# Softmax passes of an attention pipeline stand one unit later in ScalarE's and VectorE's order, between two copies of turned probabilities

## The chip, the cores and the metric

One core of a Trainium2 chip. TensorE (PE in the profile), VectorE (DVE), ScalarE (ACT), GpSimd (POOL) and SyncE (SP) each work through an instruction stream of their own, in the order in which the kernel wrote it, and wait for each other with semaphores. The metric is the device time of one execution in microseconds.

## The reference, cut to what matters

One encoder block on 1024 tokens of 1024 channels, float32. A first part mixes tokens in two attention branches with 8 heads each, a second part is a mixture of 32 experts. The attention is what the change touches:

```python
# branch B ("fox"): causal, each head has keys and values of its own
logit = jnp.einsum('bqhd,bshd->bhqs', q_blk, kb) * ATTN_SCALE
logit = logit + cq_blk - cum_t            # bias, then the causal mask
p = jax.nn.softmax(logit, axis=-1)
ob = jnp.einsum('bhqs,bshd->bqhd', p, vb)
# branch A ("dsa"): one key head and one value head for all, 256 selected keys per query
logit = jnp.where(valid, logit, NEG_INF)
p = jax.nn.softmax(logit, axis=-1)
oa = jnp.einsum('bqhk,bqkd->bqhd', p, v_sel)
```

## The kernel before

All work orders are written out by hand. The time from about 218 to 714 us is a pipeline over 64 **units**. A unit is one pair of heads (p, 0 to 3) and one block b of 128 queries, which looks at b+1 tiles of 128 keys. Units 0 to 31 are branch B, and in each pair b runs 7, 6, 5, ..., 0. Units 32 to 63 are branch A, and in each pair b runs 7, 0, 6, 1, 5, 2, 4, 3. "Block 7" below is a unit with b = 7: its rows are 1024 wide, those of block 4 are 640 wide, those of block 0 are 128 wide.

The stages of one unit are these, each for the two heads z = 0 and 1:

- scores: PE multiplies queries by keys into PSUM (L1120).
- `largest`: DVE adds bias or mask, writes the logits to SBUF and takes the row extremum (L1600, semaphore `lg_done`).
- `exps`: ACT takes the exponential in place and sums the row (L810, `p_done`).
- `inverse`: DVE takes the reciprocal of the two sums (L1607, `r_ok`).
- `scaled`: each row is multiplied by it (`n_done`), on ACT in branch B (L816), on DVE in branch A (L1614).
- turning: PE transposes the probabilities into one of two PSUM banks, in groups of two key tiles times two heads, so of up to four 128x128 tiles (L1131). Block 7 and block 6 have 4 groups, blocks 5 and 4 have 3, 3 and 2 have 2, 1 and 0 have 1.
- `turned`: ACT copies each group to SBUF (L823, `pt_copied`).
- values: PE multiplies the values by each copied group (L1145, `pv_done`).
- The output is copied from PSUM by ACT in branch B (L855) and by DVE in branch A (`out_a`, L1619, `o_done`). The first values product of the next unit waits for that.

Each engine has a loop over n from -3 to 63 (LEAD is 3), and one pass handles several units. In pass n PE issues the scores of unit n+3, then the turning of unit n, where the values of a group follow the turning of the group after it:

```python
for f in range(groups):
    turn_p(n, f)
    if f >= 1:
        values(n, f - 1)
```

Between them and the last values product PE has other work in some passes: projections of the next head pair (L1095, L1101) in units of branch B other than blocks 3 and 1 of the first three pairs, query projections and turns of branch A (L1159, L1167, rotated on DVE at L1648 to L1651) in units 24 to 32, and modulation rows (L1176, added on DVE at L1664) in units 44 to 51. The scores of a unit wait until `largest` of the unit before it is done.

In pass n ACT copies the groups of unit n. In branch B one of the two `scaled` of unit n+2 stands behind each of the first two copies. Behind the last copy stand the two `exps` of unit n+3. In passes 56 to 62 a rounding of 1024 columns follows (`high`, L843), whose counterpart on DVE is `low` (L1672, passes 57 to 63).

In pass n DVE does, in branch A, the output copy of unit n-1, `inverse` and `scaled` of unit n+2, `largest` of unit n+3, and then pieces of other work. In branch B it does `largest` of unit n+3, half of the pieces of a threshold search (L1535), `inverse` of unit n+3, and the other half. `choose` (L1635 to L1639) is such a piece, in passes 28 to 33.

Of the kernel before, what the change touches and what calls it, by code (L numbers as in the profile page):

```python
# [22 lines left out]
TT = S // P  # L23
# [48 lines left out]
LEAD = 3  # L72
# [50 lines left out]
def build(nc, x, c, positions, w_mod, b_mod, g_mix, w_in, b_forget, w_out_a, w_out_b, w_out, g_ffn,  # L123
# [11 lines left out]
    with ExitStack() as ctx:  # L135
# [315 lines left out]
        def logits(n):  # L451
            return (lg_b if n < N_B else lg_a)[n % 4]
# [265 lines left out]
        def _(act):  # L718
# [83 lines left out]
                    dst = vall[p % 2][:, 4 * half:4 * half + 4, :].rearrange("q a n -> q (a n)")  # L802
                act.activation(dst, ps[:, 7, :], ACT.Copy, scale=float(HD ** -0.5) if j == 1 else 1.0).then_inc(pj_out, 1)

            def exps(n):
                b = UNITS[n][2]
                for z in range(2):
                    buf, u = logits(n)[z][:, 0:WB[b]], 2 * (n % TT) + z
                    act.wait_ge(lg_done, 2 * n + z + 1)
                    act.activation(buf, buf, ACT.Exp, bias=nmax[:, u:u + 1], scale=-1.0, accum_out=rs[:, u:u + 1]).then_inc(p_done, 1)  # L810

            def scaled(n, z):
                b = UNITS[n][2]
                buf, u = logits(n)[z][:, 0:WB[b]], 2 * (n % TT) + z
                act.wait_ge(r_ok, n + 1)
                act.activation(buf, buf, ACT.Copy, scale=rinv[:, u:u + 1]).then_inc(n_done, 1)  # L816
# [34 lines left out]
            for n in range(-LEAD, N_U):  # L851
                if 1 <= n <= N_B:
                    _, p, b = UNITS[n - 1]
                    act.wait_ge(pv_done, GROUP_AT[n])
                    act.activation(oT[1][p][:, b * P:(b + 1) * P], ps[:, 6, 0:P], ACT.Copy).then_inc(o_done, 1)  # L855
                left = [0, 1] if 0 <= n + LEAD - 1 < N_B else []
                if n >= 0:
                    for f in range(len(key_groups(n))):
                        turned(n, f)
                        if left:  # L860
                            scaled(n + LEAD - 1, left.pop(0))
                for z in left:
                    scaled(n + LEAD - 1, z)
                if N_B - TT < n <= N_B:
                    qa_turned(n - (N_B - TT) - 1)
                if n + LEAD < N_U:
                    exps(n + LEAD)
                if -3 <= n < -1:
                    pj_evac(0, n + 7)
                elif 0 <= n < N_B - TT and n % TT in PJ_AT:  # L870
                    pj_evac(n // TT + 1, PJ_AT[n % TT])
                elif N_B - TT <= n < N_B:
                    qa_copy(n - (N_B - TT))
                if n >= N_U - TT and n - (N_U - TT) < KT - 1:
                    high(n - (N_U - TT))
# [491 lines left out]
        def _(dve):  # L1367
# [236 lines left out]
            def inverse(n):  # L1604
                u = 2 * (n % TT)
                dve.wait_ge(p_done, 2 * n + 2)
                dve.reciprocal(rinv[:, u:u + 2], rs[:, u:u + 2]).then_inc(r_ok, 1)  # L1607
# [77 lines left out]
            for n in range(-LEAD, N_U):  # L1685
                todo = parts.get(n, [])
                if n > N_B:
                    out_a(n - 1)
                if N_B - TT < n <= N_B:
                    rope_a(n - (N_B - TT) - 1)  # L1690
                if N_B <= n + LEAD - 1 < N_U:
                    inverse(n + LEAD - 1)
                    scaled(n + LEAD - 1)
                if n + LEAD < N_U:
                    largest(n + LEAD)
                half = len(todo) // 2 if n + LEAD < N_B else 0
                for piece in todo[:half]:
                    piece()
                if n + LEAD < N_B:
                    inverse(n + LEAD)  # L1700
                for piece in todo[half:]:
                    piece()
            out_a(N_U - 1)
# [242 lines left out]
```

## Time and profile before

| | |
|---|---|
| median of 3 runs | 1828.5 us (1826.37 to 1828.74) |
| the profiled execution | 1829.64 us, its span 1827.4 us |
| PE busy | 1676.7 us, 92% of the span |
| DVE busy | 961.7 us, 53% |
| ACT busy | 496.6 us, 27% |

The profiled execution's own time is its span and 2.2 us around it. The span holds, in this order, the projections (to 218 us), the pipeline of units (to 714 us), the output projections and gates, the routing, and the experts (from about 1300 us).

### The profile page before, as it was taken

The numbers are of one execution on the slowest core, as the hardware profiler recorded it, in microseconds if no ns is written. First come the engines' busy times: TensorE is split into PE (matmuls) and PEld (weight loads), VectorE is DVE, ScalarE is ACT, GpSimd is POOL, SyncE is SP. The second block draws the span as 40 slices with busy tenths as digits, with TensorE's granted clock in tenths as the row PEclk, the third lists the DMA queues.
The fourth block names the chain that finished last, engine by engine and source line by source line (L and its number), as shares of the span: only waits on it lengthen the run. The fifth ranks groups of instructions, "written<-read, shape, count | busy, mean of one in ns | idle before, by whom it ended". The sixth has DMA issues, their size and how long they took to land.

```text
span 1827.4 us, 22908 instructions
## 1 busy us (share of the span) xinstructions
PE 1676.7 (92%) x7928; PEld 857.0 (47%) x7929; DVE 961.7 (53%) x1913; ACT 496.6 (27%) x1020; POOL 191.1 (10%) x371
## 2 busy tenths in 40 slices
PE   5998889999998898999999999499999989999892
PEld 2563456564644555676666455233333333333330
DVE  5666697887877665556464433533333323333323
ACT  3214545454544655101110112011111111111112
POOL 0010000000000000000000000122222212222221
PEclk9999999999999999999999998699999999999996
DMA  9552201010000120112111813899999746999996
GB/s 353 184 187 67 70 19 40 24 47 1 1 1 2 58 70 1 35 34 69 34 34 70 324 58 109 328 357 398 378 327 400 283 126 233 395 401 368 397 400 246
DMA packets 102905, 316.63 MB, mean 173 GB/s; under 512 B 9920, under 2 KB 46824, under 8 KB 78256
## 3 DMA queue, kind: packets, MB, share of 16 engines
q1 hardware_dynamic: 91088, 287.88, 41.0%
q0 software_dynamic: 11744, 27.79, 6.3%
q8 instruction: 44, 0.72, 0.2%
q14 instruction: 29, 0.24, 0.0%
HBM read 289.14 MB, written 26.51 MB: 173 GB/s over the span
## 4 chain that ended last, share of the span: by engine, by line
PE 83%; DVE 5%; ACT 5%; DMA 4%; issue 2%; SPq 1%; POOLq 0%; POOL 0%; DVEq 0%; ACTq 0%
PE ps L1296 19%; PE ps L1222 10%; PE ps L1314 9%; PE ps L1211 6%; PE ps L1095 5%; PE ps L1257 5%; PE ps L1145 4%; PE ps L1120 4%; PE ps L1015 3%; PE ps L1159 3%; PE ps L1131 2%; PE ps L1101 2%; ACT arena L823 2%; PE ps L1053 2%; PE ps L1290 2%
## 5 line engine op out<-in xcount | busy, mean ns | idle before, releaser
L1296 PE MATMUL ps<-arena 128*64 128x512 f32 x1632 | 377.2, 605 | 17.0 <-issue 10.1
L1296 PEld LDWEIGHTS ps<-arena 128*64 128x64 f32 x1632 | 115.6, 139 | 231.7 <-issue 217.8
L1884 DVE COPY arena<-ps 128x256 f32<-128x256 f32 x51 | 21.6, 424 | 381.9 <-ACT arena L931 381.9
L1314 PE MATMUL ps<-arena 128*64 128x512 f32 x816 | 186.3, 598 | 0.6 <-DVE arena L1906 0.6
L1222 PE MATMUL ps<-rounded 128*128 128x512 f32 x768 | 183.3, 398 | 0.0
L1535 DVE TENSOR_SCALAR_CACHE_REDUCE arena<-arena,small 128x384 bf16<-128x384 f32 (+2 forms) x192 | 171.3, 939 | 0.0
L1222 PEld LDWEIGHTS ps<-rounded 128*128 128x128 f32 x768 | 144.2, 188 | 36.6 <-issue 7.7
L710 POOL DMA_INDIRECT sum_rows<-arena,ones x51 | 81.4, 1595 | 433.3 <-DVE arena L1906 422.3
L1145 PE MATMUL ps<-arena 128*64 128x128 f32 x1152 | 96.4, 286 | 23.4 <-ACT arena L823 22.4
L1211 PE MATMUL ps<-arena 128*128 128x512 f32 x256 | 112.5, 592 | 2.2 <-DVEq L1708 2.2
L1257 PE MATMUL ps<-arena 128*128 128x512 f32 x256 | 112.0, 595 | 1.9 <-DMA arena<-in_w_out_dram 1.9
L1600 DVE CUSTOM_DVE_ANT_0 arena<-ps,arena 128x896 f32<-128x896 f32 (+7 forms) x128 | 91.7, 753 | 39.9 <-PE ps L1120 37.5
L935 ACT ACTIVATE arena<-ps 128x256 f32<-128x256 f32 x51 | 19.5, 383 | 336.7 <-PE ps L1305 336.7
L823 ACT ACTIVATE arena<-ps 128x512 f32<-128x512 f32 (+1 forms) x160 | 85.4, 551 | 88.5 <-PE ps L1131 88.3
L1714 DVE RECIPROCAL arena<-arena 128x1024 f32<-128x1024 f32 x16 | 104.8, 6553 | 0.5
L810 ACT ACTIVATE arena<-arena,small 128x896 f32<-128x896 f32 (+7 forms) x128 | 97.8, 769 | 12.0 <-DVE small L1600 12.0
L1314 PEld LDWEIGHTS ps<-arena 128*64 128x64 f32 x816 | 54.3, 136 | 94.0 <-issue 88.0
L1145 PEld LDWEIGHTS ps<-arena 128*64 128x64 f32 x1152 | 59.7, 136 | 71.2 <-ACT arena L823 45.5
L1120 PE MATMUL ps<-arena 64*128 64x512 f32 (+3 forms) x384 | 81.2, 528 | 11.6 <-DVE small L1600 10.7
L1889 DVE RECIPROCAL arena<-arena 128x256 f32<-128x256 f32 x51 | 89.0, 1745 | 0.0
L1131 PE MATMUL ps<-ident,arena 128*128 128x128 f32 x576 | 88.7, 286 | 0.0
L890 ACT ACTIVATE arena<-ps 128x1024 f32<-128x1024 f32 x16 | 16.4, 1023 | 256.0 <-PE ps L1222 256.0
(297 smaller groups left out, 2012.7 us busy)
## 6 DMA issues: line engine op xcount, KB each, us to landing
arena<-in_w_e_gate_dram SPq DMA_DIRECT2D x64, 1024.0 KB
arena<-in_w_e_up_dram SPq DMA_DIRECT2D x64, 1024.0 KB
arena<-in_w_e_down_dram SPq DMA_DIRECT2D x32, 2048.0 KB
arena<-in_w_mod_dram SPq DMA_DIRECT2D x12, 2048.0 KB, 8.5
arena<-in_w_in_dram SPq DMA_DIRECT2D x32, 512.0 KB, 4.5
arena<-in_x_dram SPq DMA_DIRECT2D x16, 512.0 KB, 8.4
sum_rows<-arena SPq DMA_DIRECT2D x9, 512.0 KB, 2.6
arena<-cum_rows SPq DMA_DIRECT2D x8, 512.0 KB, 5.2
```

The costliest lines, as they stand in the source:

```text
L810: act.activation(buf, buf, ACT.Exp, bias=nmax[:, u:u + 1], scale=-1.0, accum_out=rs[:, u:u + 1]).then_inc(p_done, 1)
L823: act.activation(pT_of(n, g)[:, 0:2 * len(keys) * P], ps[:, 4 + k % 2, 0:2 * len(keys) * P], ACT.Copy).then_inc(pt_copied, 1)
L1120: m = pe.matmul(ps[:, 2 * z + a // 512, 0:e - a], q[half, b * P:(b + 1) * P], k[half, a:e], start=True, stop=True)
L1131: m = pe.transpose(ps[:, 4 + k % 2, (2 * i + z) * P:(2 * i + z + 1) * P], logits(n)[z][:, kb * P:(kb + 1) * P], ident[:])
L1145: m = pe.matmul(ps[z * HD:(z + 1) * HD, 6, 0:P], v, pT_of(n, g)[:, (2 * i + z) * P:(2 * i + z + 1) * P], start=kb == 0, stop=kb == b)
L1211: m = pe.matmul(ps[:, 4 * half + 2 + g, :], w[2 + g][:, kt, :], oT[g][kt][:, tok], start=kt == 0, stop=kt == 3)
L1222: m = pe.matmul(ps[:, 4 * half + g, :], a, b, start=kt == 0 and k == 0, stop=kt == KT - 1 and k == 2)
L1257: m = pe.matmul(ps[:, 2 * (t % 2) + n, :], mT[:, kt, t * P:(t + 1) * P], wout[:, kt, n * 512:(n + 1) * 512], start=kt == 0, stop=kt == KT - 1)
L1296: m = pe.matmul(ps[o * TB:(o + 1) * TB, 2, 0:2 * FQ].rearrange("p (j n) -> p j n", j=2), xT[:, k % NX, k // NX * TB:(k // NX + 1) * TB], w ...
L1314: m = pe.matmul(ps[o * TB:(o + 1) * TB, 5, 0:DQ], hidT[:, k % NH_T, k // NH_T * TB:(k // NH_T + 1) * TB], w_dn[c][:, k, o * DQ:(o + 1) * D ...
L1535: chain.up(dve.tensor_scalar(junk[b % 2][:, 0:WB[B0 + b]], scb[b], thr(b), None, op, ALU.add, accum_out=cnt[:, b:b + 1]))
L1714: link(dve.reciprocal(e, e))
```

## The change

ACT takes `exps` of unit n+2 instead of n+3, and in branch B `scaled` of unit n+1 instead of n+2. All four now go into one list, of which one entry is taken behind each copy of a turned group, and the rest behind the last copy. In branch A the list holds just the two `exps`. DVE takes `inverse` one unit later in branch B (n+2 instead of n+3), and in branch A its `largest` of unit n+3 now stands ahead of `inverse` and `scaled` of unit n+2. PE's order is as before, and no instruction is added or taken out.

```diff
-            def exps(n):
+            def exps(n, z):
                 b = UNITS[n][2]
-                for z in range(2):
-                    buf, u = logits(n)[z][:, 0:WB[b]], 2 * (n % TT) + z
...
-                left = [0, 1] if 0 <= n + LEAD - 1 < N_B else []
+                left = [(scaled, n + LEAD - 2, z) for z in range(2) if 0 <= n + LEAD - 2 < N_B]
+                left += [(exps, n + LEAD - 1, z) for z in range(2) if 0 <= n + LEAD - 1 < N_U]
                 if n >= 0:
                     for f in range(len(key_groups(n))):
                         turned(n, f)
                         if left:
-                            scaled(n + LEAD - 1, left.pop(0))
-                for z in left:
-                    scaled(n + LEAD - 1, z)
+                            softmax_part, m, z = left.pop(0)
+                            softmax_part(m, z)
+                for softmax_part, m, z in left:
+                    softmax_part(m, z)
                 if N_B - TT < n <= N_B:
                     qa_turned(n - (N_B - TT) - 1)
-                if n + LEAD < N_U:
-                    exps(n + LEAD)
...
-                if N_B <= n + LEAD - 1 < N_U:
-                    inverse(n + LEAD - 1)
-                    scaled(n + LEAD - 1)
                 if n + LEAD < N_U:
                     largest(n + LEAD)
-                half = len(todo) // 2 if n + LEAD < N_B else 0
+                half = len(todo) // 2 if n + LEAD - 1 < N_B else 0
                 for piece in todo[:half]:
                     piece()
-                if n + LEAD < N_B:
-                    inverse(n + LEAD)
+                if 0 <= n + LEAD - 1 < N_U:
+                    inverse(n + LEAD - 1)
+                if N_B <= n + LEAD - 1 < N_U:
+                    scaled(n + LEAD - 1)
                 for piece in todo[half:]:
                     piece()
```

In the changed kernel the lines of ACT and of DVE read one lower (L822 for L823, L809 for L810, L815 for L816, L1599 for L1600, and so on).

ACT in branch B, unit 0 (block 7). Before: four copies, the two 768-wide `scaled` of unit 2 between them, the two 640-wide `exps` of unit 3 behind them.

```order
L823 ACTIVATE arena<-ps 128x512
L816 ACTIVATE arena<-arena,small 128x768
L823 ACTIVATE arena<-ps 128x512
L816 ACTIVATE arena<-arena,small 128x768
L823 ACTIVATE arena<-ps 128x512 x2
L810 ACTIVATE arena,small<-arena,small 128x640 x2
```

The same unit in the changed kernel:

```order
L822 ACTIVATE arena<-ps 128x512
L815 ACTIVATE arena<-arena,small 128x896
L822 ACTIVATE arena<-ps 128x512
L815 ACTIVATE arena<-arena,small 128x896
L822 ACTIVATE arena<-ps 128x512
L809 ACTIVATE arena,small<-arena,small 128x768
L822 ACTIVATE arena<-ps 128x512
L809 ACTIVATE arena,small<-arena,small 128x768
```

The `scaled` between the copies are those of the unit before, one step wider, and an exponential stands ahead of the last copy.

ACT in branch A, the blocks 2, 4 and 3 of one pair of heads. Before: the copies of a unit stand together (two, then three, then two), and the `exps` of the unit three ahead behind them.

```order
L823 ACTIVATE arena<-ps 128x512
L823 ACTIVATE arena<-ps 128x256
L810 ACTIVATE arena,small<-arena,small 128x1024 x2
L823 ACTIVATE arena<-ps 128x512 x2
L823 ACTIVATE arena<-ps 128x256
L810 ACTIVATE arena,small<-arena,small 128x128 x2
L823 ACTIVATE arena<-ps 128x512 x2
```

The same units in the changed kernel:

```order
L822 ACTIVATE arena<-ps 128x512
L809 ACTIVATE arena,small<-arena,small 128x512
L822 ACTIVATE arena<-ps 128x256
L809 ACTIVATE arena,small<-arena,small 128x512
L822 ACTIVATE arena<-ps 128x512
L809 ACTIVATE arena,small<-arena,small 128x1024
L822 ACTIVATE arena<-ps 128x512
L809 ACTIVATE arena,small<-arena,small 128x1024
L822 ACTIVATE arena<-ps 128x256
```

The second and the third copy of a unit now each have an exponential ahead of them; the 1024-wide ones stand in block 4 instead of behind block 2.

DVE in branch A, pass 32 and the start of pass 33. Before: `inverse` and `scaled` of unit 34 (L1607, L1614), `largest` of unit 35 (L1600), `choose` for block 4, the output copy of unit 32 (L1619).

```order
L1607 RECIPROCAL small<-small 128x2
L1614 TENSOR_SCALAR arena<-arena,small 128x896 x2
L1600 ISA arena,small<-ps,arena 128x256
L1600 ISA small 128x1
L1600 ISA arena,small<-ps,arena 128x256
L1600 ISA small 128x1
L1635 TENSOR_SCALAR arena<-arena,small 128x640
L1636 SCALAR_TENSOR_TENSOR arena<-arena 128x640
L1637 SCALAR_TENSOR_TENSOR arena<-arena,small 128x640
L1638 SCALAR_TENSOR_TENSOR arena<-arena,small 128x640
L1639 TENSOR_SCALAR arena<-arena 128x640
L1619 COPY arena<-ps 128x128
```

The same place in the changed kernel:

```order
L1599 ISA arena,small<-ps,arena 128x256
L1599 ISA small 128x1
L1599 ISA arena,small<-ps,arena 128x256
L1599 ISA small 128x1
L1606 RECIPROCAL small<-small 128x2
L1613 TENSOR_SCALAR arena<-arena,small 128x896 x2
L1634 TENSOR_SCALAR arena<-arena,small 128x640
L1635 SCALAR_TENSOR_TENSOR arena<-arena 128x640
L1636 SCALAR_TENSOR_TENSOR arena<-arena,small 128x640
L1637 SCALAR_TENSOR_TENSOR arena<-arena,small 128x640
L1638 TENSOR_SCALAR arena<-arena 128x640
L1618 COPY arena<-ps 128x128
```

`inverse` has moved behind `largest`; it waits for `exps` of unit 34, which ACT now takes in pass 32 and took in pass 31 before.

## Rows read from the trace of the kernel before

**Rows 1.** The page: PE's busy row, the chain that ended last.

```profile
PE 1676.7 (92%) x7928; PEld 857.0 (47%) x7929; DVE 961.7 (53%) x1913; ACT 496.6 (27%) x1020; POOL 191.1 (10%) x371
PE 83%; DVE 5%; ACT 5%; DMA 4%; issue 2%; SPq 1%; POOLq 0%; POOL 0%; DVEq 0%; ACTq 0%
```

**Rows 2.** Busy time by stretch; PEclk is the granted clock (share of full speed).

```profile
247.00:568.00 321.00, 309.03 (x1774) 180.12 (x1774) 254.25 (x702) 151.14 (x338) 15.00 (x56) 1.00 0.06 17
576.00:584.00 8.00, 5.10 (x30) 3.18 (x29) 7.72 (x18) 3.52 (x7) 0.00 (x0) 0.79 0.00 0
584.00:714.00 130.00, 116.29 (x965) 70.16 (x963) 87.98 (x235) 85.52 (x189) 0.00 (x0) 1.00 0.16 46
```

**Rows 3.** PE's waits, 247 to 568 us: total, times, longest.

```profile
PE ps L1145 <- ACT arena L823: 10.3, 34, 0.7
```

**Rows 4.** PE's waits, 568 to 714 us.

```profile
PE ps L1145 <- ACT arena L823: 12.1, 30, 1.4
PE ps L1120 <- DVE small L1600: 4.1, 6, 1.8
```

**Rows 5.** ACT's groups by form, 247 to 714 us: busy us, mean ns.

```profile
L810 ACT ACTIVATE arena<-arena,small 128x1024 f32<-128x1024 f32 x14 | 15.9, 1146 | 0.6 <-DVE small L1600 0.6
L810 ACT ACTIVATE arena<-arena,small 128x512 f32<-128x512 f32 x16 | 11.3, 712 | 0.0
```

**Rows 6.** Timeline, unit 8 (block 7, branch B): start us, length us.

```profile
324.11 1.09 PE L1131 MATMUL ps<-ident,arena 128*128 128x128 f32 x8
...
324.80 0.60 ACT L823 ACTIVATE arena<-ps 128x512 f32<-128x512 f32 x1 [1.47 <-PE ps L1131]
...
326.12 0.59 ACT L823 ACTIVATE arena<-ps 128x512 f32<-128x512 f32 x1
...
326.76 0.66 PE L1145 MATMUL ps<-arena 128*64 128x128 f32 x8
```

**Rows 7.** Timeline of PE, branch A: blocks 4 and 7, no other work between.

```profile
674.97 1.09 PE L1131 MATMUL ps<-ident,arena 128*128 128x128 f32 x8
...
677.32 0.98 PE L1145 MATMUL ps<-arena 128*64 128x128 f32 x12
678.23 1.77 PE L1120 MATMUL ps<-arena 64*128 64x512 f32 x8
...
682.99 1.09 PE L1131 MATMUL ps<-ident,arena 128*128 128x128 f32 x8
...
686.68 1.42 PE L1145 MATMUL ps<-arena 128*64 128x128 f32 x16
```

**Rows 8.** Timeline of DVE, passes 30 and 31.

```profile
552.29 0.62 DVE L1635 TENSOR_SCALAR arena<-arena,small 128x768 f32<-128x768 f32 x1
...
558.75 0.29 DVE L1648 TENSOR_TENSOR arena<-arena,small 128x128 f32<-128x128 f32 x1 [1.34 <-ACT arena L829]
```

**Rows 9.** Timeline, passes 32 to 34.

```profile
569.61 1.09 ACT L823 ACTIVATE arena<-ps 128x512 f32<-128x512 f32 x2 [0.82 <-PE ps L1131]
569.72 1.28 DVE L1614 TENSOR_SCALAR arena<-arena,small 128x896 f32<-128x896 f32 x2
...
571.60 0.55 DVE L1635 TENSOR_SCALAR arena<-arena,small 128x640 f32<-128x640 f32 x1
...
577.01 0.95 DVE L1600 CUSTOM_DVE_ANT_0 arena<-ps,arena 128x768 f32<-128x768 f32 x1
...
579.00 1.65 PE L1120 MATMUL ps<-arena 64*128 64x384 f32 x4 [1.79 <-DVE small L1600]
...
583.01 0.66 PE L1145 MATMUL ps<-arena 128*64 128x128 f32 x8 [0.64 <-ACT arena L823]
```

**Rows 10.** Timeline, passes 61 and 62.

```profile
706.16 0.17 DVE L1607 RECIPROCAL small<-small 128x2 f32<-128x2 f32 x1 [0.39 <-ACT arena L810]
...
708.53 0.29 DVE L1619 COPY arena<-ps 128x128 f32<-128x128 f32 x1 [0.15 <-PE ps L1145]
...
709.76 0.66 PE L1145 MATMUL ps<-arena 128*64 128x128 f32 x8 [0.25 <-ACT arena L823]
```

More of the change, by code:

```diff
@@ L803, in pj_evac @@
                 act.activation(dst, ps[:, 7, :], ACT.Copy, scale=float(HD ** -0.5) if j == 1 else 1.0).then_inc(pj_out, 1)
-            def exps(n):
+            def exps(n, z):
                 b = UNITS[n][2]
-                for z in range(2):
-                    buf, u = logits(n)[z][:, 0:WB[b]], 2 * (n % TT) + z
-                    act.wait_ge(lg_done, 2 * n + z + 1)
-                    act.activation(buf, buf, ACT.Exp, bias=nmax[:, u:u + 1], scale=-1.0, accum_out=rs[:, u:u + 1]).then_inc(p_done, 1)
+                buf, u = logits(n)[z][:, 0:WB[b]], 2 * (n % TT) + z
+                act.wait_ge(lg_done, 2 * n + z + 1)
+                act.activation(buf, buf, ACT.Exp, bias=nmax[:, u:u + 1], scale=-1.0, accum_out=rs[:, u:u + 1]).then_inc(p_done, 1)
             def scaled(n, z):
```

## The prediction, made before the changed kernel ran

> **What bounds the kernel now.** I read the page first. PE is busy for 92% of the span and holds 83% of the chain that ended last [rows 1], so a delay counts where it holds up PE. Busy time by stretch gives what there is to win in the pipeline of units: PE is busy 309.0 of 321 us in branch B, and 116.3 of 130 us from 584 to 714 us [rows 2], so it idles 12.0 and 13.7 us, at the full granted clock of 1.00. The list of waits names the causes: PE waits for ACT's copies 34 times for 10.3 us in branch B [rows 3], and 30 times for 12.1 us after 568 us, where six waits for DVE's `largest` add 4.1 us [rows 4]. Most of the copy waits are the way from a turning to its copy and back, which has nothing to do with `exps`.
>
> The timelines show that way. T is the start of a unit's turning. In unit 8, T = 324.11, the first copy starts at T + 0.69 (324.80), the second at 326.12, and the values product on the second starts at 326.76 [rows 6], 0.64 after its copy starts. Between the two copies lie 1.32 us: one copy slot (0.49; two together take 1.09 [rows 9], the second running its whole 0.60) and one 768-wide `scaled` of 0.83. So product k starts at the earliest at
>
> T + 0.69 + 0.64 + k × (0.49 + E), or T + 1.33, 1.82 + E, 2.31 + 2E,
>
> where E is what stands between two copies. Where nothing does, PE sets the pace itself: in branch A's block 7 the third product starts 3.69 us after T (682.99 to 686.68) [rows 7], some 1.18 us a group after the first. So E is free up to about 0.69 us for one and adds up over two.
>
> **The change, part by part.** No instruction is added. What counts is where ACT and DVE are when PE needs them.
>
> *exps behind the last copy (before).* In branch A, PE has 2.5 to 3.5 us between two units' copies (last products, scores, next turning), and the two `exps` fit there: 2 × 1.146 us at 1024 columns, 2 × 0.712 at 512 [rows 5], so 0.108 us per block of 128 columns.
>
> *exps between copies, branch A (after).* E is now an `exps` of unit n+2:
> - Block 7, E = 1.04 (896 wide): third product at 2.31 + 2.08 = 4.39 instead of 3.69, +0.7 us. Three such units besides unit 32: 2.1.
> - Block 6, E = 0.93: 4.17 for 3.69, +0.5, three times besides unit 34: 1.5.
> - Block 5, E = 0.82: 3.95 against about 3.25 (its third product follows the second directly), +0.7 in units 36 and 52; +0.1 in 44, where the modulation matmul (about 1.1 us) stands ahead of the last product; nothing in 60: 1.5.
> - Block 4, E = 1.146 (1024): its last group is half as long, so its copy signals some 0.2 earlier. Last product at 2.31 + 2.29 − 0.2 = 4.4, next scores 0.4 later, T + 4.8. Before they start at T + 3.26 (674.97 to 678.23), and the products are issued in one run from 677.32 [rows 7]. +1.5 in units 38 and 54, +0.7 in 46 behind the modulation: 3.7.
> - Block 3, E = 0.39: second product at 2.21 for 1.93, +0.3 twice: 0.6. Block 2, E = 0.71: most of the delay is hidden, since the scores behind it wait for a 1024-wide `largest` anyway; +0.2 twice: 0.4. Blocks 1 and 0 have one group, so nothing stands between copies.
>
> Sum 9.8 us.
>
> *scaled one step wider between copies, branch B.* Blocks 7 and 6: E grows by 0.108, the third product comes 0.2 later, eight times: 1.7. Block 3 +0.1 in three pairs, block 5 0.04 four times: 0.4. The exponential ahead of block 7's last copy costs nothing: the 7 us projection (L1095, L1159) stands between the third product and the last. Without this cover it would cost about 0.9 a time. Blocks 4, 2, 0 have the same cover. Sum 2.1 us.
>
> *DVE waits for exps inside a pass.* In branch A, DVE's queue behind `inverse` holds `scaled`, the pieces, and then the next pass's output copy, for which PE's first product waits.
> - Pass 30: `exps` of unit 32 (1024 wide) now end some 4.2 us after T (copy, two 128-wide `scaled`, two `exps`). `inverse`, `scaled` and `choose` follow, so `choose` starts at 555.2, not at 552.29. DVE has 1.34 us of idle ahead of the next rotation (558.75) [rows 8], and PE needs that rotation about 0.9 us after its end. 2.9 − 1.3 − 0.8 leaves 0.8 us.
> - Pass 32: ACT's first copy starts at 569.61; the second `exps` (896) ends at 569.61 + 2 × (0.49 + 1.04) = 572.7. With 0.2 for the signal and 1.45 for `inverse` and `scaled` (1.28 of it the row at 569.72), `choose` starts at 574.3 instead of 571.60 [rows 9], 2.7 late. `largest` of unit 36 passes `scaled` of unit 35 (0.8), so it is 1.9 late (578.9 for 577.01), and the scores at 579.00 with it. Behind the next `choose` the output copy is 2.8 late, and the product at 583.01 with it [rows 9]. This swallows the delays of units 32 and 34. 2.8 us.
> - Passes 57 to 62, with `low` (1.2 us) behind `scaled`: unit 57 gains 0.2, because ACT's rounding no longer follows a 768-wide `exps`. In pass 59 `low` now comes behind the 384-wide `exps` and `scaled`, and the output copy holds up the first product of unit 60 by 0.5. In pass 61 the last `exps` (512) stand between the copies, so `inverse`, which started at 706.16, starts about 7.6 us after unit 60's T instead of 4.7. `scaled` (0.9) and `low` follow, and the output copy of unit 61 comes at about 9.9; the first product of unit 62 starts at 10.2 instead of 8.3 (709.76) [rows 10]. Sum 2.2 us.
>
> *What could be won.* ACT's and DVE's mutual waits shrink, but PE waits for neither of them there. The ceiling is the 4.1 us for `largest` [rows 4]; most of it is bound to scores that PE itself has just issued.
>
> **Sum.** 9.8 + 2.1 + 0.8 + 2.8 + 2.2 = 17.7 us, on the profiled execution's 1829.6 us: 1847.3. The median is 1.1 us lower, so I give 1846.5 us. After 714 us the output projections follow on PE at once, so I let all of it through.
>
> The Trainium skill, "Perfetto Trace Analysis", section "Optimization Strategy", says that where the most-contended engine changes, interleaving the regimes may help. The page's own rows do not show such a change here: PE is the busier engine in both branches [rows 2]. By that rule the ACT work spread among the copies would cost nothing or gain, which is the first or third rival below; by the rows it costs 17.7 us.
>
> **The rivals.**
> - *Hidden anyway.* PE's third product waits, but the loss is caught up because later PE work was waiting for something else, such as `largest` or a weight transfer. For it: swallowed delays as in unit 34. Against it: 13.7 us of PE idle in 130 us [rows 2] is too little to absorb 14 us, most of it being the fixed way of a copy. Time 1828 to 1831 us.
> - *Only the steady part.* The per-unit delays (11.9 us) come, those on DVE do not, because ACT runs ahead: 1840.5 us. And the other way: a long PE wait lowers the clock. It was granted 0.79 in the 8 us around the 1.79 us wait at 579.00 [rows 2, 4]. Those 8 us cost about 1.8 us at the lower level; three more such places give 1852 us.
> - *Faster.* `largest` ahead of `inverse` and `scaled` lets PE's scores start earlier, and `exps` never wait. At its most, all of the 4.1 us [rows 4], with the copy waits above 0.25 us at blocks 1 to 3 another 4: 1820 us. It decides if E between copies turns out below 0.69 us, so that no product waits. Against it: the 1.32 us between copies at 324.80 and 326.12 are in the trace [rows 6], and the `exps` are wider than that `scaled`.
>
> The Trainium skill, same page, section "Tensor Engine Instruction", calls ACT and DVE strict first-in first-out. The rows agree: the copy at 326.12 starts 0.83 after a slot's 0.49, though its turning had ended long before. If ACT could let a copy pass, the sum would fall to nearly 0.
>
> **How the numbers follow.** Own forecast, slower by 8 to 27 us: 0.82. Hidden: 0.07, mostly within 0.2% (3.7 us, about what a measurement of this kernel can tell from no change). Faster by more than 0.2%: 0.06. Slower still than 1857: 0.05. The range of the first case is 1836.5 to 1857: below, half the delays; above, one and a half times, which takes in the clock. Outside lie 2 in 10. Chances: faster 0.06, same 0.06, slower 0.88.
>
> **What would show it.** Per branch A block 7, third product at T + 4.4; block 4, next scores at T + 4.8; PE's waits for L822 from 22.4 us up to about 35; DVE's wait at `inverse` longer in passes 30 and 32 (about 2.5 us each), the product at 583 late by 2.8; the first product after the pipeline about 18 us late. Wrong would be: products that start at their old distance from T, or an attention stretch as long as before.

## The result: 18.6 us slower, and the profile after

The changed kernel takes 1845.99 us (median of 4 runs, 1844.7 to 1850.59) against 1827.43 us (median of 4, 1825.48 to 1828.74): a ratio of 1.0113 with a 95% interval of 1.0089 to 1.0138 (the two medians alone give 1.0102). Forecast were 1846.5 us and a range of 1836.5 to 1857 us.

The page of the changed kernel, with the rows that answer to [rows 1]:

```profile
PE 1678.8 (91%) x7928; PEld 857.1 (47%) x7929; DVE 962.7 (52%) x1913; ACT 492.5 (27%) x1020; POOL 191.5 (10%) x371
PE 81%; DVE 6%; ACT 5%; DMA 3%; issue 3%; SPq 1%; ACTq 0%; POOLq 0%; POOL 0%; DVEq 0%
```

PE is busy for 2.1 us more than before (1678.8 for 1676.7 us). The other 13.3 of the 15.4 us by which the profiled span grew (1842.8 for 1827.4) are time in which PE did nothing. Busy time by stretch of the changed kernel; each row gives the stretch and its length, then the busy time of PE, PE's weight loads, DVE, ACT and POOL, each with its instructions, then the granted clock, the share of the DMA engines and GB/s:

```profile
247.00:568.00 321.00, 306.86 (x1748) 178.06 (x1745) 251.12 (x690) 148.33 (x337) 15.01 (x56) 1.00 0.06 17
585.00:728.00 143.00, 119.74 (x972) 71.44 (x968) 88.41 (x236) 83.66 (x189) 0.00 (x0) 0.99 0.15 41
```

In branch B PE idles 14.1 of 321 us (12.0 before, [rows 2]); from 585 to 728 us, branch A's larger part, it idles 23.3 us, where it idled 13.7 in the 130 us from 584 to 714. The waits of PE in the changed kernel, 569 to 745 us, answer to [rows 4]:

```profile
PE ps L1144 <- ACT arena L822: 18.5, 49, 1.5
PE ps L1144 <- DVE arena L1618: 7.8, 5, 2.3
PE ps L1119 <- DVE small L1599: 3.0, 4, 1.3
```

Each row gives who waited for whom, the total in us, how often, and the longest. The waits for ACT's copies went from 12.1 to 18.5 us, and there is a cause that was not in the list before: 7.8 us for DVE's output copy (L1618, L1619 in the numbering of before). Part of the 18.5 us belongs elsewhere: a wait for two semaphores is put down to the one that came last, and the longest of this row, 1.48 us in unit 52, was for DVE too:

```profile
675.20 0.60 ACT L822 ACTIVATE arena<-ps 128x512 f32<-128x512 f32 x1 [1.31 <-PE ps L1130]
675.51 1.22 DVE L1667 SCALAR_TENSOR_TENSOR arena<-arena 128x1024 f32<-128x1024 f32 x1
...
676.65 0.28 DVE L1618 COPY arena<-ps 128x128 f32<-128x128 f32 x1
...
677.08 0.66 PE L1144 MATMUL ps<-arena 128*64 128x128 f32 x8 [1.48 <-ACT arena L822]
```

The first copy of the unit had ended at 675.80. What ended just before the product at 677.08 was the output copy (676.93), which stood behind a late piece of 1.22 us (L1667). The second copy, from 676.50 to 677.08, is the row that the view names. In the kernel that takes the list up one copy later (below), where no exponential stands between these two copies, the same product waits 1.49 us, and there the row names DVE. So some 17 us of the waits are for copies and 9.3 us for the output copy.

To see where the time came in, I took the start of `largest` of each unit from both timelines (`largest` of unit n runs in pass n-3) and subtracted that of unit 0. What the changed kernel had lost by then, in us:

| up to `largest` of unit | lost in all | in this stretch | forecast for it |
|---|---|---|---|
| 32 (branch B) | 2.5 | 2.5 | 2.1 |
| 36 (passes 30 to 32) | 5.2 | 2.7 | 0.8 + 1.9 |
| 40 | 7.8 | 2.65 | 0.9 + 0.7 |
| 60 | 16.4 | 8.6 | 8.6 |
| last product of unit 63 | 18.3 | 1.9 | 0.5 + 2.2 |

What lies outside the pipeline is not put down to the change. Unit 0's `largest` started at 222.04 us before and at 217.53 after, 4.5 us earlier. In the first 60 us the granted clock was 0.94 in the one profile and 1.00 in the other, and over eleven kernels with the same instructions up to there the start lay between 216.15 and 222.63 us. Behind the last product the changed kernel took 1.6 us more; from 728 to 745 us its granted clock was 0.90, and 1.00 in the kernel before from 714 to 731. 18.3 − 4.5 + 1.6 = 15.4 us, the difference of the spans. The medians differ by 18.6 us. That the start averages out over their runs would fit, but is not shown, since only one execution of each kernel was profiled.

**Between the copies.** Timeline of the changed kernel, block 4 (T = 684.63) and block 7 (T = 694.49) of branch A, the counterparts of [rows 7]:

```profile
684.63 1.09 PE L1130 MATMUL ps<-ident,arena 128*128 128x128 f32 x8
...
685.32 0.60 ACT L822 ACTIVATE arena<-ps 128x512 f32<-128x512 f32 x1 [0.84 <-PE ps L1130]
...
685.82 1.14 ACT L809 ACTIVATE arena<-arena,small 128x1024 f32<-128x1024 f32 x1
...
686.95 0.58 ACT L822 ACTIVATE arena<-ps 128x512 f32<-128x512 f32 x1
687.43 1.14 ACT L809 ACTIVATE arena<-arena,small 128x1024 f32<-128x1024 f32 x1
...
688.99 0.44 PE L1144 MATMUL ps<-arena 128*64 128x128 f32 x4 [0.74 <-ACT arena L822]
689.36 1.78 PE L1119 MATMUL ps<-arena 64*128 64x512 f32 x8
...
694.49 1.09 PE L1130 MATMUL ps<-ident,arena 128*128 128x128 f32 x8
...
698.85 1.15 PE L1144 MATMUL ps<-arena 128*64 128x128 f32 x16 [0.26 <-ACT arena L822]
```

Block 4's last product starts at T + 4.36 (4.4 forecast) and the next scores at T + 4.73 (4.8 forecast, 3.26 before). Block 7's third product starts at T + 4.36 (4.39 forecast, 3.69 before). Read down ACT's rows: copy, exponential, copy, exponential, with no idle between them: the exponential of 685.82 hands over to the copy at 686.95, and that one to the exponential at 687.43. PE waits at the end of each pair.

**DVE in passes 30 to 34.** Timeline of the changed kernel:

```profile
553.21 0.62 DVE L1634 TENSOR_SCALAR arena<-arena,small 128x768 f32<-128x768 f32 x1
...
558.36 0.29 DVE L1647 TENSOR_TENSOR arena<-arena,small 128x128 f32<-128x128 f32 x1
...
559.30 0.66 PE L1166 MATMUL ps<-ident,arena 128*128 128x128 f32 x4 [0.63 <-DVE arena L1650]
...
571.60 0.17 DVE L1606 RECIPROCAL small<-small 128x2 f32<-128x2 f32 x1 [2.47 <-ACT arena L809]
...
573.00 0.55 DVE L1634 TENSOR_SCALAR arena<-arena,small 128x640 f32<-128x640 f32 x1
...
577.92 0.44 PE L1144 MATMUL ps<-arena 128*64 128x128 f32 x4 [2.12 <-DVE arena L1618]
...
579.67 0.92 PE L1119 MATMUL ps<-arena 64*128 64x384 f32 x4 [1.31 <-DVE small L1599]
...
584.42 1.12 PE L1144 MATMUL ps<-arena 128*64 128x128 f32 x8 [2.26 <-DVE arena L1618]
```

`inverse` waits 2.47 us for `exps` in pass 32. Ahead of the rotation at 558.36 DVE has no idle time left (1.34 us before, [rows 8]), and PE waits 0.63 us for it. In pass 33 the first product waits 2.12 us for the output copy and the scores behind it 1.31 us for `largest`; in pass 34 the first product waits 2.26 us for the output copy.

**The tail.** Timeline of the changed kernel, passes 61 and 62, as [rows 10]:

```profile
721.02 0.17 DVE L1606 RECIPROCAL small<-small 128x2 f32<-128x2 f32 x1 [1.54 <-ACT arena L809]
...
723.15 0.28 DVE L1618 COPY arena<-ps 128x128 f32<-128x128 f32 x1
...
723.59 0.66 PE L1144 MATMUL ps<-arena 128*64 128x128 f32 x8 [1.78 <-DVE arena L1618]
```

### The profile page after: what moved, and what is told of

Same layout as the page of the kernel before. It is cut to its first block, busy times and chain, and to the rows that moved or that the text cites. A ratio compares the mean times of both kernels' runs of the same rounds, so it can differ in the third digit from the quotient of the medians.

```text
span 1842.8 us, 22907 instructions
## 1 busy us (share of the span) xinstructions
PE 1678.8 (91%) x7928; PEld 857.1 (47%) x7929; DVE 962.7 (52%) x1913; ACT 492.5 (27%) x1020; POOL 191.5 (10%) x371
## 4 chain that ended last, share of the span: by engine, by line
PE 81%; DVE 6%; ACT 5%; DMA 3%; issue 3%; SPq 1%; ACTq 0%; POOLq 0%; POOL 0%; DVEq 0%
PE ps L1295 19%; PE ps L1221 9%; PE ps L1313 9%; PE ps L1210 6%; PE ps L1094 5%; PE ps L1256 4%; PE ps L1119 4%; PE ps L1144 3%; PE ps L1014 3%; PE ps L1158 3%; PE ps L1100 2%; PE ps L1130 2%; ACT arena L822 2%; PE ps L1052 2%; PE ps L1289 2%
## 5 line engine op out<-in xcount | busy, mean ns | idle before, releaser
L1295 PE MATMUL ps<-arena 128*64 128x512 f32 x1632 | 379.2, 607 | 16.1 <-issue 10.2
L1599 DVE CUSTOM_DVE_ANT_0 arena<-ps,arena 128x896 f32<-128x896 f32 (+7 forms) x128 | 91.7, 754 | 49.6 <-PE ps L1119 46.4
L1210 PE MATMUL ps<-arena 128*128 128x512 f32 x256 | 114.2, 600 | 2.2 <-DVEq L1706 2.2
L822 ACT ACTIVATE arena<-ps 128x512 f32<-128x512 f32 (+1 forms) x160 | 87.1, 550 | 106.8 <-PE ps L1130 106.8
L1256 PE MATMUL ps<-arena 128*128 128x512 f32 x256 | 112.0, 595 | 2.1 <-DMA arena<-in_w_out_dram 2.1
L809 ACT ACTIVATE arena<-arena,small 128x896 f32<-128x896 f32 (+7 forms) x128 | 98.2, 770 | 0.0
L1119 PE MATMUL ps<-arena 64*128 64x512 f32 (+3 forms) x384 | 80.5, 524 | 10.2 <-DVE small L1599 9.5
L1094 PE MATMUL ps<-arena 128*128 128x512 f32 x192 | 85.6, 599 | 0.0
```

The source lines that it names most:

```text
L822: act.activation(pT_of(n, g)[:, 0:2 * len(keys) * P], ps[:, 4 + k % 2, 0:2 * len(keys) * P], ACT.Copy).then_inc(pt_copied, 1)
L1094: m = pe.matmul(ps[:, 7, :], wB[j][:, kt, :], hT[:, kt, half * 512:(half + 1) * 512], start=kt == 0, stop=kt == KT - 1)
L1119: m = pe.matmul(ps[:, 2 * z + a // 512, 0:e - a], q[half, b * P:(b + 1) * P], k[half, a:e], start=True, stop=True)
L1210: m = pe.matmul(ps[:, 4 * half + 2 + g, :], w[2 + g][:, kt, :], oT[g][kt][:, tok], start=kt == 0, stop=kt == 3)
L1256: m = pe.matmul(ps[:, 2 * (t % 2) + n, :], mT[:, kt, t * P:(t + 1) * P], wout[:, kt, n * 512:(n + 1) * 512], start=kt == 0, stop=kt == KT - 1)
L1295: m = pe.matmul(ps[o * TB:(o + 1) * TB, 2, 0:2 * FQ].rearrange("p (j n) -> p j n", j=2), xT[:, k % NX, k // NX * TB:(k // NX + 1) * TB], w ...
```

## The experiments

Since the start of the pipeline lay up to 6.5 us apart in the profiles, each experiment is read by its medians and by its own pipeline: from `largest` of unit 0 to the start of the last products, which took 490.9 us before and 509.3 us in the changed kernel (+18.3). The pipeline's length comes from one profile a kernel. It contains what the granted clock cost there, which differed from profile to profile: stretches at the lower of its two levels (1.2 GHz for 2.4) cost at most 1.7 us in branch A in the kernel before and 3.4 us in the changed one. The names of the functions are those of the printed code.

### The parts alone: branch B, branch A

Both kernels choose by unit m whether its `exps`, `scaled` and `inverse` stand as before or as changed (the lines shown are ACT's; DVE's order is chosen in the same way).

```diff
+LATE = lambda m: m < N_B - 2          # the other kernel: m >= N_B
-                left = [(scaled, n + LEAD - 2, z) for z in range(2) if 0 <= n + LEAD - 2 < N_B]
-                left += [(exps, n + LEAD - 1, z) for z in range(2) if 0 <= n + LEAD - 1 < N_U]
+                left = [(scaled, m, z) for m in (n + LEAD - 2, n + LEAD - 1)
+                        if 0 <= m < N_B and LATE(m) == (m == n + LEAD - 2) for z in range(2)]
+                left += [(exps, n + LEAD - 1, z) for z in range(2) if 0 <= n + LEAD - 1 < N_U and LATE(n + LEAD - 1)]
...
+                if n + LEAD < N_U and not LATE(n + LEAD):
+                    exps(n + LEAD, 0)
+                    exps(n + LEAD, 1)
```

> Only branch B has the new order (units 0 to 29); units 30 to 63 and DVE's order in branch A are as before. Own theory: a wider scaled between the copies of blocks 7, 6, 5 and 3 is all that costs, +2.1 us on the kernel before, about 1829.5 (ratio 1.001), and from pass 30 on each unit keeps its old distances. Rival, lateness itself costs (a unit's probabilities come too late for its turning): several us already here, with first turnings of a unit waiting for scaled. Rival, a late exps helps ACT in branch B: below the kernel before.

Measured: 1829.91 us (12 runs) against 1827.81, ratio 1.0013 (0.9999 to 1.0027). Its pipeline had lost 2.5 us by unit 36 and 3.9 us by unit 40, and nothing after that. The 2.5 us are branch B's own, and the same as in the changed kernel. The other 1.4 us fall into the stretch where the granted clock was 0.79 and then 0.89 in this kernel, and 0.83 and then 1.00 before (below). The medians say +2.1 us, as forecast, but by their interval no difference can't be ruled out; the timeline is the firmer evidence.

> Only units 32 to 63 have the new order, on ACT and on DVE; branch B is as before. Own theory: 9.8 us between copies, 0.8 and 2.8 us at passes 30 and 32, 2.2 us in the tail, so +15.6 us and, with the slow clock at pass 33 that the changed kernel shows, up to +17: about 1843 to 1845. Rival, the two branches interact (branch B's delays push branch A's): then this run and the one with branch B alone do not add up to the whole change.

Measured: 1845.57 us, ratio 1.0102 (1.0074 to 1.013), and a pipeline 16.4 us longer. So branch A carries most of the loss. 16.4 + 3.9 is 2.0 us more than the 18.3 of the whole. At passes 32 to 35 the granted clock was 0.79 in 10 us and 0.75 in the next 12 us here, which costs at most 5.1 us, and the kernel with branch B alone paid up to 3.4 us there, the whole 3.4 and the kernel before 1.7. So the two parts together contain up to 3.4 us more of the lower clock than the whole does, which is enough for the 2.0. An interaction of the branches isn't needed for it, though it isn't ruled out.

### Late, but behind the copies

The changed kernel, with the list of branch A taken up only behind the last copy:

```diff
                         turned(n, f)
-                        if left:
+                        if left and n < N_B:
```

> The changed kernel, but in branch A both exps stand behind the last copy of a unit (still of unit n+2, still one unit late, DVE as changed). Own theory: the waits of PE for copies fall back to their old size (about 12 us after 585 us, for 17.7), but exps now end 2 to 3 us later after a unit's T, so DVE reaches the output copy late: blocks 7 and 4 lose about 1 us each on it, block 6 0.3, pass 32 5.5 instead of 2.8. In sum 1843 to 1849, hardly better than the changed kernel, with the waits for L1618 grown in place of those for L822. Rival, only the place between the copies costs: then 9.8 us come back, about 1836.

Measured: 1859.67 us, ratio 1.0177 (1.0148 to 1.0206), pipeline +31.7 us. Slower than both theories said. Its waits of PE, 569 to 745 us:

```profile
PE ps L1144 <- DVE arena L1618: 20.9, 13, 5.4
PE ps L1119 <- DVE small L1599: 9.2, 11, 1.2
PE ps L1144 <- ACT arena L822: 3.9, 13, 0.5
```

The kind of wait is as my theory had it: the 18.5 us for ACT's copies shrank to 3.9, and 20.9 us for the output copy stand in their place. The size is not, for two reasons. One is the second row of this table, which I had overlooked: DVE's next `largest` stands behind the late output copy, and PE's next scores wait for it (9.2 us, 3.0 in the changed kernel). The other is the clock. Busy time from `largest` of unit 32 to the last products, of the changed kernel and then of this one:

```profile
537.45:726.79 189.34, 158.28 (x1148) 91.43 (x1148) 124.71 (x309) 102.64 (x241) 0.00 (x0) 0.98 0.11 31
538.03:740.50 202.47, 165.42 (x1149) 97.22 (x1149) 122.77 (x309) 105.20 (x240) 0.00 (x0) 0.93 0.11 29
```

Of the 13.1 us by which this stretch is longer, PE idles 6.0 us, and for 7.1 us it is busy longer with the same products, at a granted clock of 0.93 for 0.98. So less than half of the difference from the changed kernel is waiting; the rest goes with the lower clock (0.77 from 620 to 642 us, 0.71 from 724 to 741).

The timeline of this kernel in block 4 and behind it:

```profile
609.23 1.14 ACT L809 ACTIVATE arena<-arena,small 128x1024 f32<-128x1024 f32 x1
...
610.49 0.17 DVE L1606 RECIPROCAL small<-small 128x2 f32<-128x2 f32 x1 [3.65 <-ACT arena L809]
...
612.02 0.28 DVE L1618 COPY arena<-ps 128x128 f32<-128x128 f32 x1
...
612.45 1.09 PE L1144 MATMUL ps<-arena 128*64 128x128 f32 x16 [1.03 <-DVE arena L1618]
...
614.38 0.70 PE L1119 MATMUL ps<-arena 64*128 64x256 f32 x4 [0.83 <-DVE small L1599]
```

So lateness has a price of its own at this place: `exps` of unit n+2, in the pass in which DVE wants its sums, holds up DVE, and DVE holds up PE. In the changed kernel the place between the copies keeps that price small, and costs PE waits for copies instead.

### Between the copies, but not late

The kernel before, with the two `exps` of unit n+3 behind the first and the second copy in branch A:

```diff
+                early = [(0,), (1,)] if n + LEAD < N_U else []
...
                             scaled(n + LEAD - 1, left.pop(0))
+                        elif n >= N_B and early:
+                            exps(n + LEAD, early.pop(0))
```

> The kernel before, but in branch A the two exps of unit n+3 (no unit late, DVE as before) stand behind the first and the second copy. Own theory: ACT also has to wait there for largest of the same pass, so that exps holds up the copies of blocks 7 (0.15), 6 (0.8), 5 (1.1), 4 (0.7), 3 (1.1) and 2 (0.8 us): 4.6 us per pair of heads, 12 to 16 us in all, 1840 to 1844, with no extra wait for DVE's output copy at pass 34. Rival, lateness is what costs and place is harmless: within 2 us of the kernel before.

Measured: 1847.08 us, ratio 1.0105 (1.0078 to 1.0133), pipeline +17.3 us; some 3 us above what was expected. Its waits of PE, 569 to 745 us:

```profile
PE ps L1148 <- ACT arena L823: 25.1, 48, 1.6
...
PE ps L1148 <- DVE arena L1622: 2.1, 1, 2.1
```

The waits for copies doubled (25.1 for 12.1 us) with no unit late. The theory by which the place between the copies is harmless falls. But this run does not price the length of the exponentials alone: they also wait there for `largest` of the same pass, and hold up the copy behind them for that time. ACT waits 14.0 us for `largest` in this stretch, where it waited 2.1 us before. Pass 34 shows it:

```profile
585.18 0.62 ACT L810 ACTIVATE arena<-arena,small 128x384 f32<-128x384 f32 x1 [3.50 <-DVE small L1603]
...
585.79 0.58 ACT L823 ACTIVATE arena<-ps 128x512 f32<-128x512 f32 x1
...
586.42 1.12 PE L1148 MATMUL ps<-arena 128*64 128x128 f32 x8 [1.62 <-ACT arena L823]
```

I had not expected the 2.1 us wait for the output copy in pass 34. Why it comes is not shown; `exps` stands later than before there, though not by a whole pass, and it may be that DVE's `choose` pass feels it.

### DVE's work in passes 28 to 33 spread out

`choose` is five instructions for each of six blocks. Here they are handed out as 5, 6, 6, 7, 4 and 2 over the passes 28 to 33 instead of five each, in the kernel before and in the changed one:

```diff
-            for n, b in CHOOSE_AT.items():
-                parts.setdefault(n, []).append(lambda b=b: choose(b - B0))
+            for n, count_of in CHOOSE_STEPS.items():
+                for b, step in [next(choose_order) for _ in range(count_of)]:
+                    parts.setdefault(n, []).append(lambda b=b, step=step: choose(b - B0, step))
```

> The kernel before, with the thirty instructions of choose handed out over passes 28 to 33 as 5, 6, 6, 7, 4, 2 instead of five a pass, so that the idle time of DVE in passes 29 to 31 (2.0, 1.3 and 3.2 us) takes about 2.2 us of them out of passes 32 and 33. Theory: the scores that waited 1.79 us for largest in pass 34 start about 1.4 us earlier, the clock does not fall there (0.79 in 8 us, 1.8 us lost), the output copy no longer holds up unit 34: 3 to 4 us faster, about 1824.5. Rival: these waits were cover for others and the time stays within 1 us.

Measured: 1826.47 us against 1828.28, ratio 0.9991 (0.9977 to 1.0005): no difference by the interval, and well short of the 3 to 4 us expected. The pipeline became 1.5 us shorter, all of it between units 32 and 40. The 1.4 us for DVE came; the clock did not stay up (0.83 in the 10 us behind the same place).

> The changed kernel with the same handing out of choose. Theory: the part of the loss that hangs on DVE in passes 30 to 34 (0.8 us, 2.8 us and the slow clock) shrinks by 3 to 5 us, so 1841 to 1843; the 9.8 us between the copies and the tail stay. Rival, that part was not DVE's: no change from the changed kernel (1846).

Measured: 1844.09 us, ratio 1.009 (1.0065 to 1.0114), pipeline +15.2 us, 3.1 less than the changed kernel's. Up to unit 40 it had lost 3.8 us instead of 7.8. So some 4 us of the loss hang on DVE's load in passes 30 to 34. The same spreading gave the kernel before 1.4 us there. Half of the 4 us is not waiting: from `largest` of unit 32 to that of unit 40 PE idles 7.4 us here and 9.5 us in the changed kernel, and it is busy 50.8 for 52.8 us, with a granted clock of 1.00 for 0.95.

### One copy later

If a product waits only for what stands ahead of its own copy, the free place is between the second and the third copy, where ACT idles. This is the changed kernel with that place, and then the kernel before (where the list holds `scaled` alone) with the same edit:

```diff
                         turned(n, f)
-                        if left:
+                        if left and f >= 1:
```

> The changed kernel with the list taken up one copy later: a scaled or exps stands behind the second and the third copy of a unit, none behind the first. Theory (a product starts at T + 1.33 + what ACT has to do ahead of its copy, and ACT idles between the second and the third copy, 0.95 us from T + 1.67 to 2.62): of the 9.8 us between copies in branch A about 1.2 are left (block 7 0.1, block 4 0.35), branch B falls 2 us below the kernel before, the DVE terms stay or grow by 0.5 (exps of block 7 and 4 end later). In sum +6 us on the kernel before, about 1834.5, 11 us below the changed kernel. Rival, lateness alone costs (as in the run with all exps behind the copies): no better than the changed kernel, 1846 or above, with the waits moved to DVE's output copy.

Measured: 1833.77 us against 1829.14, ratio 1.0029 (1.0014 to 1.0044), 12 us below the changed kernel's median, with every unit as late as there. Its pipeline is 8.2 us longer than before, where some 6 us were expected, and 10.1 us shorter than the changed kernel's. Its waits of PE, 568 to 730 us:

```profile
PE ps L1144 <- DVE arena L1618: 10.3, 8, 3.3
PE ps L1144 <- ACT arena L822: 9.6, 27, 0.7
PE ps L1119 <- DVE small L1599: 4.5, 9, 1.1
```

The waits for copies are below those of the kernel before (9.6 for 12.1 us), in part because eight products that waited for a copy before now wait for the output copy. What is left of the loss is DVE's for the most part: 10.3 us for the output copy. From 570 to 580 us the granted clock was 0.55, and the lower level lasted about 10 us, so up to 5.1 us of this pipeline are the clock's.

The 10.1 us are not all branch A's. 5.6 us of them came by unit 32, in branch B, and 4.5 us behind it. Read by single units, from one turning to the next, the cost between the copies is gone where nothing else holds up PE: 0.65 us in unit 36, 0.66 in units 46 and 48 and 0.67 in unit 50 went to 0, and 1.47 us in units 38 and 54 (block 4) to 0.35, as expected. The 1.23 us of unit 52 stayed to the hundredth, which is how I know that they were DVE's.

> The kernel before, with the two scaled of branch B behind the second and the third copy instead of the first and the second. Theory: product 2 of blocks 7 and 6 and product 1 of block 3 no longer wait for ACT (0.27, 0.07 and 0.3 us a time): 2.3 us less in the pipeline, about 1825.5. Rival: nothing, since the waits of PE for copies in branch B are the fixed way only.

Measured: 1824.54 us against 1829.14, ratio 0.9981 (0.9964 to 0.9998), pipeline 3.5 us shorter, all of it in branch B. This is the fair counterpart of the run above: with the list one copy later in both, the change still costs 9.2 us by the medians and 11.7 us by the pipelines, nearly all in branch A, up to 3.4 of them by the clock.

> The one before this with choose handed out as 5, 6, 6, 7, 4, 2. Theory: both gains add, 2.3 and 1.5 us: about 1824, ratio 0.998. Rival: the slow clock at passes 32 to 34 comes and goes from run to run and hides it.

Measured: 1823.02 us against 1829.14, ratio 0.9965 (0.995 to 0.9981), pipeline 4.8 us shorter. This version is faster than both kernels, though by little: both its edits are to the order of before, with the two `scaled` one copy later and `choose` spread out.

## Why the prediction was right

- **Between the copies, branch A, 9.8 us.** Right in kind, and the size came out nearer than the terms did. Where no other work of PE stands ahead of them, the products start within 0.1 us of T + 1.33 + k × (0.49 + E) (third product at T + 4.36 in block 7, 4.14 in block 6, 3.93 in block 5), except in units 33, 34, 52 and 60 to 62, which wait for DVE's output copy. That the waits for the copies go unit by unit when the same work stands one copy later shows the cause. But that the loss from unit 40 to unit 60 was 8.6 us, just the 8.6 of the sum, is partly luck. Block 7 cost 0.4, 0.66 and 0.4 us in units 40, 48 and 56, where I had 0.7 each: in two of them its last product came only 0.4 us later. Unit 52 cost 1.23 us where I had 0.7 for its copies: that was DVE's output copy, a wait which the sum did not have in this pass. Block 3 cost 0.37 a time for 0.3, since its second product came at T + 1.83 before and not at the 1.93 that I had.
- **Wider `scaled`, branch B, 2.1 us.** 2.5 us in the timelines of both kernels that have it. The way was right. The difference is block 4, which I had as covered and which costs 0.1 us each of four times. The same formula also holds for the kernel before, whose own price at that place I put at 2.3 us and which is 3.5: block 6 gives back 0.28 us a time there, for which I had 0.07, and block 3 0.39 for 0.3.
- **Passes 30 and 32, 0.8 and 2.8 us.** The first two arrivals (2.7 us by unit 36) are as forecast. From there to unit 40 the loss was 2.65 us for 1.6. The missing term is most likely the clock, which I had only as an extra. Busy time by stretch of the changed kernel, two stretches that start 354 and 364 us after unit 0's `largest`, the second 12 us long:

```profile
571.50:581.50 10.00, 6.31 (x48) 3.80 (x47) 9.62 (x18) 3.23 (x11) 0.00 (x0) 0.97 0.00 0
581.50:593.50 12.00, 9.05 (x65) 5.47 (x64) 7.44 (x20) 5.52 (x13) 0.00 (x0) 0.74 0.01 2
```

The same two of the kernel before:

```profile
576.00:586.00 10.00, 7.10 (x52) 4.43 (x51) 8.80 (x22) 4.87 (x10) 0.00 (x0) 0.83 0.00 0
586.00:598.00 12.00, 10.39 (x84) 6.08 (x82) 8.32 (x23) 7.22 (x19) 0.00 (x0) 1.00 0.34 121
```

And of the changed kernel with `choose` spread out:

```profile
576.00:586.00 10.00, 7.46 (x62) 4.53 (x64) 8.83 (x21) 4.75 (x13) 0.00 (x0) 1.00 0.00 0
586.00:598.00 12.00, 9.84 (x94) 6.19 (x90) 6.98 (x23) 7.76 (x19) 0.00 (x0) 1.00 0.13 32
```

By the granted clock the kernel before lost at most 10 × 0.17 = 1.7 us there, the changed one 10 × 0.03 + 12 × 0.26 = 3.4 us, 1.7 more, and the spread-out one nothing. (At most, since a clock that is low while PE idles costs nothing. PE's busy time from unit 32 to unit 40 grew by 0.9 us.) But the share is not a fixed one: with branch B alone changed, the same instructions as before ran there at 0.79 and 0.89. What decides how long the lower of the two levels (1.2 GHz for 2.4) stays, these runs leave open.
- **The tail, 0.5 + 2.2 us.** 1.9 us measured, 0.8 less than forecast. The chain was the forecast one, with 1.78 us of waiting for the output copy in pass 62, and the first product of unit 62 starts 10.09 us after unit 60's T (10.2 forecast). What I had left out is a wait that became shorter: the first product of unit 61 waited 1.37 us for its copy before, and 0.73 us for the output copy now.
- **PE's waits for the copies** were to go from 22.4 to about 35 us. They came to 30.3: 11.8 in branch B, where they were 10.3, and 18.5 behind it. The mark was too high. It was the 22.4 us and the 11.9 us of the terms between copies. But five products that had waited 3.0 us for a copy before (the first ones of units 33, 34, 60, 61 and 62) now wait for the output copy, and stand in the 7.8 us.
- **What could be won.** Nothing was: no stretch of the table became shorter. The rival "faster" had named the right criterion (E below 0.69 us). The kernel before, shifted, shows that there is a cheaper place for an E, but it is one copy later.
- **The Trainium skill** ("Perfetto Trace Analysis", "Optimization Strategy": interleaving regimes may improve performance). Here PE is the busier engine throughout, so the page's case isn't this one; what the runs show is that spreading ACT's work between the copies cost 18.3 us of pipeline at one place and 8.2 us at the next. The rule of the strict first-in first-out queues (same page, "Tensor Engine Instruction") agrees with the ACT rows shown: the copy of block 4 at 686.95 starts 1.13 us behind the exponential at 685.82, which is 1.14 us long, and in the run that puts `exps` between the copies without being late a copy stands behind an exponential that waited 3.50 us.

What I had wrong is in the experiments: the run with `exps` behind the copies was to take 1843 to 1849 us and took 1859.7, since I followed DVE's delay to the output copy and not on to `largest` and the scores behind it, and had no term for the clock. In the changed kernel that branch is small (3.0 us of waits for `largest`, 4.1 before), so the error hardly touched the prediction.

## What to carry to other kernels

When helper work stands between the small steps of a pipeline on an engine that runs in order, write down for each step when the bound engine needs it, and put the work where the helper would idle: here the same list of `exps` and `scaled` made the pipeline 18.3 us longer behind the first and the second copy, and 8.2 us behind the second and the third. Compare like with like, too: the kernel before also gained 3.5 us from that place, so moving the softmax later by a unit still cost 11.7 us there. Moving work later by a stage is not free, because the next engine's queue behind it (a reciprocal, then an output copy, then the next logits) moves with it; follow such a chain until it comes back to the bound engine. And compare a stage by its own length in the timeline, since the time ahead of it varied by 6.5 us here, as much as many edits bring. Then split that length into the bound engine's waiting and its busy time: in the run with `exps` behind the copies more than half of the difference from the changed kernel was busy time at a lower clock.

## What the runs showed of the hardware that was not expected

- The start of the pipeline, behind instructions that did not change, lay at 216.15 to 222.63 us in eleven profiles, and the granted clock sorts them. With 0.94 in the first 60 us and 0.93 from 120 to 170 us it lay at 221.8 to 222.6 us (five profiles, the kernel before among them, at 222.04); with 0.97 in both at 219.2; with 0.97 and 1.00 at 217.8; with 1.00 and 0.97 at 217.5 to 217.8 (three, the changed kernel at 217.53 among them); and with 1.00 in both at 216.15.
- At passes 32 to 36 the clock stood at its lower level for about 3 us in the kernel before, 7 us in the changed one and 10 us in the changed one with the list one copy later. PE's longest waits there were 1.79, 2.26 and 3.27 us. But the length of the wait does not settle it: with `choose` spread out, a longest wait of 1.06 us in the kernel before went with about 3 us at the lower level, and 1.31 us in the changed one with none. By the granted clock this cost between nothing and 5.1 us.
